# Gates asked for four blocks ahead, in four buffers, in the attention stages of a two-layer kernel

## The reference, cut to what matters

```python
oa = forgetting_attention(q, k, v, fa + b_fgate)     # softmax(q k / 8 + cum - cum) v
oa = oa * jax.nn.silu(za)
ob = sliding_window_sink_attention(qb, kb, vb, sinks)
ob = ob * jax.nn.silu(zb)
...
a = dsa_attention(...)                               # second block
a = a * jax.nn.silu(gate_a)
```

## Time and profile before

| | us |
|---|---|
| three runs | 3535.0, 3542.2, 3544.0; median 3542.2 |
| profiled execution, first to last instruction (span) | 3534.2 |
| busy in the span: PE, DVE, ACT, POOL | 3215.7, 2204.2, 1407.9, 895.6 |
| stage `f_` (683 to 1400 of the span): PE busy, DVE busy | 650.3, 505.6 of 717 |
| stage `n_` (2700 to 3340): PE busy, DVE busy | 569.3, 527.3 of 640 |

### The profile page before, as it was taken

How to read it: one execution, slowest core, us unless ns; L and a number is a source line. 1 busy time by engine, 2 the same in 40 slices (tenths; PEclk the granted TensorE clock), 3 DMA queues, 4 the chain that set the end, 5 groups by cost and what they waited for, 6 DMA issues and landing times. The chain is left out here.

```text
span 3534.2 us, 43584 instructions
## 1 busy us (share of the span) xinstructions
PE 3215.7 (91%) x15232; PEld 2466.9 (70%) x15232; DVE 2204.2 (62%) x4305; ACT 1407.9 (40%) x2383; POOL 895.6 (25%) x828
## 2 busy tenths in 40 slices
PE   4999999889999997997889999997896899999798
PEld 4799888656666665876667887886784566666576
DVE  7111011267767776332389998995773689998766
ACT  5000001134444445212258998342554233333454
POOL 0111111257455460000421333344231211211000
PEclk9999999899999998998899999998998899999999
DMA  5322223466555533436311335364133523422444
GB/s 208 105 82 73 86 83 118 127 137 144 120 130 114 115 83 118 133 122 236 79 42 44 101 110 175 107 174 157 72 115 116 163 57 70 97 62 54 130 147 134
DMA packets 331916, 400.80 MB, mean 113 GB/s; under 512 B 100324, under 2 KB 249188, under 8 KB 319124
## 3 DMA queue, kind: packets, MB, share of 16 engines
q1 hardware_dynamic: 260376, 299.09, 29.7%
q10 hardware_dynamic: 67488, 78.03, 7.2%
q0 software_dynamic: 3840, 20.98, 2.5%
HBM read 265.39 MB, written 132.62 MB: 113 GB/s over the span
## 5 line engine op out<-in xcount | busy, mean ns | idle before, releaser
L2229 PE MATMUL f_pO<-f_PT,f_vv 128*128 128x512 f32 (+3 forms) x944 | 377.2, 481 | 19.7 <-ACT f_PT L2259 19.7
L2259 ACT ACTIVATE f_PT<-f_pS 128x512 f32<-128x512 f32 (+3 forms) x472 | 221.2, 472 | 325.3 <-PE f_pS L2197 152.8
L2890 DVE TENSOR_SCALAR_CACHE_REDUCE sharedI<-xI,TI 128x768 bf16<-128x768 f32 (+10 forms) x276 | 339.5, 1296 | 5.4 <-DVE TI L2896 5.2
L2694 PE MATMUL cbank<-hT_high,cw_hi 128*128 128x512 f32 x800 | 319.7, 400 | 19.9 <-DVE cw_lo L2849 6.8
L2259 ACT ACTIVATE n_PT<-n_pS 128x512 f32<-128x512 f32 (+4 forms) x352 | 176.6, 504 | 363.0 <-PE n_pS L2209 199.2
L583 PE MATMUL p_bank<-hT_high,p_w_hi 128*128 128x512 f32 (+1 forms) x768 | 304.9, 397 | 16.1 <-DVE p_w_lo L706 16.1
L2694 PE MATMUL cbank<-hT_low,cw_hi 128*128 128x512 f32 x800 | 316.7, 396 | 0.0
L2694 PE MATMUL cbank<-hT_high,cw_lo 128*128 128x512 f32 x800 | 316.3, 395 | 0.0
L2229 PE MATMUL n_pO<-n_PT,n_vv 128*128 128x512 f32 (+4 forms) x704 | 308.3, 519 | 0.0
L583 PE MATMUL p_bank<-hT_low,p_w_hi 128*128 128x512 f32 (+1 forms) x768 | 303.6, 395 | 0.0
L583 PE MATMUL p_bank<-hT_high,p_w_lo 128*128 128x512 f32 (+1 forms) x768 | 302.7, 394 | 0.0
(11 more groups left out here) (421 smaller groups left out, 7412.9 us busy)
## 6 DMA issues: line engine op xcount, KB each, us to landing
f_zz<-scratch_z ACTq DMA_DIRECT2D x128, 128.0 KB, 3.1
c_w_first<-in_w_in_dram SPq DMA_DIRECT2D x26, 512.0 KB, 4.5
cw_raw<-in_w_in_dram SPq DMA_DIRECT2D x25, 512.0 KB, 4.4
p_w_raw<-in_w_in_dram SPq DMA_DIRECT2D x22, 512.0 KB, 3.8
lent<-scratch_qkb POOLq DMA_DIRECT2D x40, 256.0 KB, 10.3
scratch_z<-p_stage ACTq DMA_DIRECT2D x32, 256.0 KB, 2.4
scratch_qk_high<-p_stage ACTq DMA_DIRECT2D x32, 256.0 KB, 2.6
scratch_qk_low<-p_stage_low ACTq DMA_DIRECT2D x32, 256.0 KB, 3.2
```

What stands on the lines that cost most here:

```text
L2229: pe.matmul(pO[:, B % 2, c0:c1], lhsT=vv[0:nk, b, kt, :], rhs=PT[0:nk, u % PR, c0:c1], start=(kt == 0 and not heads[h].local), stop=(heads ...
L2259: act.activation(PT[0:nk, u % PR, c0:c1], pS[0:nk, u % SR, c0:c1], ACT.Exp, scale=0.125).then_inc(s_ex, 1)
L2694: last = pe.matmul(bank[:, p % RING, 0:wd], lhsT=w_part[pw][b][:, c, :], rhs=rhs, start=(c == 0 and a == 0), stop=(c == DC - 1 and a == 2))
L2890: own_.up(v.tensor_scalar(junk_v[:, own_.at % 2, 0:(i + 1) * P], scores(i), T[:, j:j + 1], None, compare, ALU.add, accum_out=count[:, j:j ...
```

## The change

`zz` gets four buffers (`GATES`), and the exponential is written over z in the upper half, so `ez` goes. The gate of block B + 4 is asked for four steps behind the end of block B; ahead of the first unit four gates are asked for instead of two. The load has to wait for both readers of its buffer now, `weight` and `times_gate`. In `f_`, `G` and its semaphores get four buffers (`OUTS`) as well; in `n_` `G` keeps two. In modulation the sixteen semaphores of the x tiles become eight, each used twice, for which the loads of groups 2 and 3 wait for the squares of groups 0 and 1 first.

```diff
                 if g == 2:
                     sp.wait_ge(s_wused, DC)
+                    sp.wait_ge(s_ssq, 4)
                 if g == 3:
                     sp.wait_ge(s_tr, DC)
+                    sp.wait_ge(s_ssq, 8)
...
-    HALF = QB4 // 2
+    HALF, GATES, OUTS = QB4 // 2, 4, 4 if rel is None else 2
...
-        zz, ez = (m.sb(n_(x), [P, 2, QB4]) for x in ("zz", "ez"))
-        w, oz, G = (m.sb(n_(x), [P, 2, HALF]) for x in ("w", "oz", "G"))
+        zz = m.sb(n_("zz"), [P, GATES, QB4])
+        w, oz = (m.sb(n_(x), [P, 2, HALF]) for x in ("w", "oz"))
+        G = m.sb(n_("G"), [P, OUTS, HALF])
...
             def load_gate(B):
                 h, j = sw.blocks[B]
-                if B >= 2:
-                    act.wait_ge(s_oz, B - 1)
+                if B >= GATES:
+                    act.wait_ge(s_w, B - GATES + 1)
+                    act.wait_ge(s_oz, B - GATES + 1)
                 for half in (lower, upper):
-                    act.dma_start(zz[half, B % 2], heads[h].z[:, j * QB4:(j + 1) * QB4]).then_inc(s_z[B % 2], 16)
+                    act.dma_start(zz[half, B % GATES], heads[h].z[:, j * QB4:(j + 1) * QB4]).then_inc(s_z[B % GATES], 16)
...
-                act.wait_ge(s_z[B % 2], 32 * (B // 2) + 32)
-                if B >= 2:
-                    act.wait_ge(s_w, B - 1)
-                act.activation(ez[upper, B % 2], zz[upper, B % 2], ACT.Exp, scale=-1.0).then_inc(s_ez, 1)
+                act.wait_ge(s_z[B % GATES], 32 * (B // GATES) + 32)
+                act.activation(zz[upper, B % GATES], zz[upper, B % GATES], ACT.Exp, scale=-1.0).then_inc(s_ez, 1)
...
-            load_gate(0)
-            load_gate(1)
+            for B in range(GATES):
+                load_gate(B)
...
-                if ended(u, 2) is not None and ended(u, 2) + 2 < NBL:
-                    load_gate(ended(u, 2) + 2)
+                if ended(u, 4) is not None and ended(u, 4) + GATES < NBL:
+                    load_gate(ended(u, 4) + GATES)
...
-                if B >= 2:
-                    v.wait_ge(s_st[B % 2], 32 * (B // 2))
+                if B >= OUTS:
+                    v.wait_ge(s_st[B % OUTS], 32 * (B // OUTS))
```

More of the change, by code:

```diff
@@ L123, in stage_modulate @@
         s_w = [m.sem(f"a_w_ada_loaded{i}") for i in range(4)]
-        s_x = [m.sem(f"a_x_loaded{i}") for i in range(NT)]
+        s_x = [m.sem(f"a_x_loaded{i}") for i in range(NT // 2)]
         s_const = m.sem("a_constants_made")
@@ L150, in load_x @@
                     sp.wait_ge(s_wused, DC)
+                    sp.wait_ge(s_ssq, 4)
                 if g == 3:
                     sp.wait_ge(s_tr, DC)
+                    sp.wait_ge(s_ssq, 8)
                 for t in range(4 * g, 4 * g + 4):
-                    sp.dma_start(rows(t), x[t * P:(t + 1) * P, :]).then_inc(s_x[t], 16)
+                    sp.dma_start(rows(t), x[t * P:(t + 1) * P, :]).then_inc(s_x[t % 8], 16)
             for k in range(4):
@@ L189, in square @@
             def square(t):
-                act.wait_ge(s_x[t], 16)
+                act.wait_ge(s_x[t % 8], 16 * (t // 8) + 16)
                 if t >= 1:
@@ L1842, in stage_attend @@
         s_v = [m.sem(n_(f"values_loaded{b}")) for b in range(NB)]
-        s_z = [m.sem(n_(f"gates_loaded{b}")) for b in range(2)]
+        s_z = [m.sem(n_(f"gates_loaded{b}")) for b in range(GATES)]
         s_max, s_mx = m.sem(n_("max_scores")), m.sem(n_("max_taken"))
@@ L1848, in stage_attend @@
         s_norm = m.sem(n_("output_gated"))
-        s_st = [m.sem(n_(f"output_stored{b}")) for b in range(2)]
+        s_st = [m.sem(n_(f"output_stored{b}")) for b in range(OUTS)]
         if rel is not None:
@@ L1945, in store @@
                     at = j * QB4 + z * HALF
-                    sp.dma_start(heads[h].g[:, at:at + HALF], G[half, B % 2]).then_inc(s_st[B % 2], 16)
+                    sp.dma_start(heads[h].g[:, at:at + HALF], G[half, B % OUTS]).then_inc(s_st[B % OUTS], 16)
             def load_masks(j):
@@ L1986, in _ @@
                         sp.dma_start(to, src).then_inc(loaded, 16)
-            for b in range(2):
-                sp.wait_ge(s_st[b], 16 * NBL)
+            for b in range(OUTS):
+                sp.wait_ge(s_st[b], 32 * (NBL // OUTS))
         @block.gpsimd
@@ L2368, in weight @@
                 for half, at in two_halves():
-                    last = v.scalar_tensor_tensor(w[half, B % 2], ez[upper, B % 2, at], 1.0, pO[upper, B % 2, at],
+                    last = v.scalar_tensor_tensor(w[half, B % 2], zz[upper, B % GATES, at], 1.0, pO[upper, B % 2, at],
                                                   ALU.add, ALU.mult)
@@ L2373, in times_gate @@
             def times_gate(B):
-                v.wait_ge(s_z[B % 2], 32 * (B // 2) + 32)
+                v.wait_ge(s_z[B % GATES], 32 * (B // GATES) + 32)
                 for half, at in two_halves():
-                    last = v.tensor_tensor(oz[half, B % 2], pO[lower, B % 2, at], zz[lower, B % 2, at], ALU.mult)
+                    last = v.tensor_tensor(oz[half, B % 2], pO[lower, B % 2, at], zz[lower, B % GATES, at], ALU.mult)
                 last.then_inc(s_oz, 1)
@@ L2384, in finish @@
                 v.wait_ge(s_oz, B + 1)
-                if B >= 2:
-                    v.wait_ge(s_st[B % 2], 32 * (B // 2))
+                if B >= OUTS:
+                    v.wait_ge(s_st[B % OUTS], 32 * (B // OUTS))
                 own_.settle()
-                v.tensor_tensor(G[:, B % 2], oz[:, B % 2], w[:, B % 2], ALU.mult).then_inc(s_norm, 1)
+                v.tensor_tensor(G[:, B % OUTS], oz[:, B % 2], w[:, B % 2], ALU.mult).then_inc(s_norm, 1)
             own_.up(v.memset(KA[0][HD:P, :].bitcast(F32), 0.0))
```

## The result

The changed kernel takes 3507.8 us in the median of five runs (3505.3 to 3514.4) against 3542.2 of before (3533.8 to 3544.0): a ratio of 0.9909, interval 0.9896 to 0.9922, which is 28 to 37 us less.

What follows compares the result with a forecast made beforehand. PE, busy in 91% of the 3534.2 us span, was taken as the bound. The terms -6.7 - 14.3 - 3.0 + 2.3 = -21.7 us took the median of 3542.2 to 3520.5, range 3510 to 3534.

Steps and rivals of the forecast that it cites:

- The gates in the local heads (gain 14.3): In f_, gates asked for earlier end ACT's waits behind local heads and PE's gaps; 6.6 + 7.7 = 14.3 us gained.
- The base: Whole kernel: the runs' median lies 8.0 us above the profiled span of 3534.2, carried over unchanged to the forecast.
- The store, the start and POOL (net -6.7): Early f_: no stall for the first head's store gains 10.95, later start costs 2.1, waiting for POOL 2.1.
- the wait of 2.1: At f_'s first local head, PE, now earlier, waits 2.1 us for POOL's KA, itself 2.5 late.
- POOL's room: At f_'s first local head, POOL has KA ready 9.2 us before PE wants it, which caps the gain there.
- The rival by which the starts cost nothing: At both attentions' starts the new loads fit beside the others; -26.5 us, time 3515.7; chance 0.15.
- The end of f_ (gain 3.0): The last gate and last store no longer hold f_'s end; gain between 1.8 and 4.1, taken as 3.0 us.
- The start of n_ (cost 2.3): 512 KB more of gate loads ahead in n_ make DVE's second mask late; cost 2.3 us, 0 to 4.6.
- Edits at nothing: The exponential in place, the stage-end semaphore waits and modulation's reused semaphores cost nothing.
- DVE did not become the bound: Rival in the local heads: DVE becomes the bound, giving back half of 14.3; gain 14.5, time 3527.7; chance 0.15.
- no pair of gates held a start for 6.6 us: Slower rival: at both starts each extra gate pair holds SP's loads 13.5 us; +27.5, time 3569.7; chance 0.03.
- gates are not late any more: Rival in the local heads: gates land later than 15.3 us, waits stay; -4.4 us, time 3537.8; chance 0.07.

Runs made afterwards that it cites:

- pauses_back: The changed kernel with eight spare exponentials on ACT at the first block of five plain heads that follow a local one; 3528.4 us, ratio 0.9950.
- base_fourth: The kernel before, unchanged, in a fourth profile; span 3534.4 us.
- stores_only: The kernel before with four buffers of G and nothing else of the change; ratio 0.9974, 9.2 us less.
- late_preload: The changed kernel with two gates asked for at the start of both attentions, the third and fourth at the fourth and sixth unit; ratio 0.9913.
- early_weights: The changed kernel with the loads of w_out asked for earlier, behind the stores of the second block of the last head but one; ratio 0.9912.
- both_moves: The changed kernel with w_out's loads asked for earlier and, in n_ alone, the third and fourth gate at the fourth and sixth unit; ratio 0.9896.
- the two parts alone: The kernel before with only four buffers of G, 0.9974; the changed kernel with two buffers of G in the first attention, 0.9958.
- base_third: The kernel before, unchanged, in a third profile; the clock falls at two of the five places.

## Why the prediction was wrong

**The step that failed is "The gates in the local heads (gain 14.3)".** Its mechanism held: ACT's waits are gone, the stretches behind local heads are all near 43 us, and the five together took 229.9 us in the first profile and 215.5 after, 14.4 less, as worked out. But 229.9 was one execution's number. Over six profiles of before they take 236.8 in the mean, so the gain is 21.3 and not 14.3: a pause of 2 to 6 us went with a fall of the granted clock to 0.5 in 20 of 30 cases, and in that execution in one of five. The forecast saw this once, at the long gap ("since PE comes back slowly from so long a pause"), and took it for a matter of long pauses; `pauses_back` shows it at 2.8 us. The Trainium skill, TensorE: Matmul & The Clock Gate, section "HAM oscillation — how this bites in real kernels", says that PE may fall to the lower clock where it waits for DMAs between bursts, and counts half of the time spent there as lost. By that a fall of 6.8 us would cost an estimated 3.4; the stretches agree (48.1 to 48.7 against 44.5 to 45.4). The bounds failed with the value: 7.2 to 17.3 were taken from the same rows.

**The base.** "the median of the runs lies 8.0 above the span and I carry that over" treats as constant what is not: the changed kernel's median lies 2.3 below its first span. Of the 8.0, 2.1 is the same in every run (time less span); the other 5.9 said that the profiled execution was shorter than most, but not where. That it is near the 6.2 by which the third line lies below its mean is chance: `base_fourth` has as short a span, 3534.4, with four falls and 625.4 in the third line, and is shorter elsewhere.

**The store, the start and POOL (net -6.7): measured -6.6,** the first two lines of the table. That is luck, since the parts were off against each other. The store gave 9.4 (`stores_only`) and not 10.95: DVE's wait for it, 10.49 in the first profile, is 9.3 to 9.7 in the other five, where PE comes to it some 1 us later. The last piece of `KL` landed 22.5 us behind the stage's first load, 20.3 before: 2.3 later, where 2.5 was worked out from bytes. But the start then cost 2.8 us, not 2.1, by PE's products ahead of the stall against the stage's first load (means of six and three profiles; 3.7 in the first pair), since the clock came back later: the stretch at 0.5 around the stage's start is 27.3 us in the first profile, 27.3 or 30.7 in the others of before, 34.1 after. PE's clock in the same window, before and after:

```profile
706.00:710.00 4.00, 3.94 (x17) 2.62 (x17) 2.60 (x6) 2.09 (x4) 3.19 (x3) 0.83 1.00 209
```

```profile
706.00:710.00 4.00, 4.00 (x14) 2.95 (x13) 1.69 (x4) 1.29 (x3) 3.20 (x4) 0.50 1.05 202
```

So PE was late enough not to meet POOL, and the wait of 2.1 wasn't there. The mechanism of POOL's room is shown by `stores_only` and `late_preload`, where PE does wait for it. The rival by which the starts cost nothing is out: `late_preload` got the 2.5 us back.

**The end of f_ (gain 3.0): measured 1.6,** under the lower bound of 1.8. The last `G` is ready 3.7 us earlier behind the landmark at 1382.40, near the full 4.1, but the loads of `w_out` still took 15.0 us from first issue to last landing, as before; the 256 KB of gates that left the queue didn't shorten them, and the stores land behind them (`early_weights`).

**The start of n_ (cost 2.3): measured 2.7.** Where the two extra pairs are asked for later it is gone in one profile (`both_moves`) and mostly there in another (`late_preload`), so the order of the loads as its cause isn't shown. **Edits at nothing:** modulation moved nothing; PE's first product of the projection stands at 91.84 and 91.83.

**The rivals.** DVE did not become the bound (43 us); no pair of gates held a start for 6.6 us; gates are not late any more.

**What stays open.** With the means of the table, what the change touches gives +1.8 - 8.4 - 21.8 - 1.6 + 2.7 = -27.3; all timed runs say -31.8 (the first ones -28 to -37). Some 5 us are in no profile, and the two parts alone, 9.2 and 14.9, add up to 24. The profiled executions of before lie 3 us below the median of their timed runs in the mean, those of the changed kernel 4 above; 3.4 of these 7 us stand in the stages that the change doesn't touch (1329.2 and 1332.7). A part of it is the clock again. By the mean clock on record (52 of the 57 runs of before, all 11 of the changed kernel), the timed runs of before were at 0.5 for 280 us in the mean and their profiles for 277, those of the changed kernel for 253 and 260. That is 10 us at 0.5 between the two comparisons, at half speed an estimated 5 us at most. Whether chance alone chose these executions wasn't settled.

## What to carry to other kernels

A wait that starves PE for two or three microseconds costs more than itself when the clock falls behind it, and one profile may show the lucky case: take two or three profiles of the kernel before, and price a pause with and without the fall. A median that lies well above its profiled execution is a reason to take more profiles before carrying the difference over; it doesn't say where the difference is. And a lead is to be measured against the burst that the load lands behind, not against its typical landing: ACT had the late gates 8 to 12 us after it asked, where the median landing was 3.1; three buffers were enough for that, and no longer when another burst was moved beside the last gates.

## What the runs showed of the hardware

- Five pauses of PE of 2.79 to 2.80 us in one execution: the granted clock fell to 0.5 for 6.8 us in two, for 3.4 us right behind one, and stayed at 1.00 at two (`pauses_back`).
- A late gate's two loads of 128 KB landed 8.0 and 8.4 us behind their issue (`base_third`, the first of the five places), among eight loads of 256 KB that POOL had issued 1.6 to 5.0 us earlier; the median landing of a gate is 3.1 us.
- Four loads more on ACT's queue, 512 KB, put off the last piece of SP's `KL` by 2.3 us. The Trainium skill, DMA: Bandwidth & Descriptors, section "Issuing engines are not separate DMA queues", would have it so.
